# The router of a two-layer decoder step: order of the evictions, and nine constant matmuls a layer

## The chip, the cores and the metric

The kernel runs on one core of one Trainium2 chip. The metric is the device time of one execution in microseconds; lower is better. PE is the matmul engine (TensorE), DVE the vector engine, ACT the scalar engine, POOL GpSimd, SP the engine that issues most of the loads. TensorE's clock has two levels, 1.2 and 2.4 GHz; the profile gives the granted clock as a share of 2.4 GHz (1.00 or 0.50, a mean in between for a stretch that holds both).

## The reference

A decoder trunk of two layers works on 288 tokens (256 of a prompt, 32 of eight sample streams), 1024 channels wide, all in float32. Each layer has a recurrent mixer, a cross-attention into 256 memory tokens, and a mixture of experts; each is followed by a residual and a LayerNorm. The part around the change is the end of the attention and the router of the experts:

```python
x = layer_norm(DN_ALPHA * x + memory_attention(x, mem_k[l], mem_v[l], w_mq[l], w_mo[l]), ln_g[l, 1], ln_b[l, 1])
...
grp_logits = xt @ w_grp + b_grp                 # 4 groups, the best one is taken
e_logits = einsum('nd,gde->nge', xt, w_er) + b_er   # 8 experts of that group, the best two are taken
...
hid = silu(xt @ w_gate) * (xt @ w_up)           # for each expert, 1024 to 512
out = out + (hid * combine) @ w_down            # 512 to 1024
```

There are 32 experts in a layer, with 6 MB of weights each.

## The kernel before

One program holds a block for each engine; they meet by semaphores that count up. Tokens lie in three tiles: tiles 0 and 1 are the prompt (128 rows each), tile 2 the 32 sample rows. The router takes them in the order 2, 0, 1 (`ORDER`).

*From the projection to the logits.* PE's `project_out` multiplies the attention's output by its weights into PSUM banks 0 to 4. DVE's `norm` then takes each tile in order: residual, mean and variance (L1427, L1429), a first step (L1430), and, once ACT has given the reciprocal root of the variance (ACT's `norm`, L1163 and L1164), the second step (L1432), which raises `ln_done`. PE's `logits(l, t)` turns tile t with transposes into PSUM banks 6 and 7 (`run_jobs`, L641, two jobs for each tile, half the channels each), ACT copies each half to `XT` (`empty_jobs`, L1056), and PE multiplies `XT` by the router's weights (L908). A job may begin when the copy of the job two before it is done, and ahead of the last tile's logits PE waits for all the copies of the stage.

ACT works its instructions in the order in which they are written. Before, it does the roots of all three tiles (`norm(2 + 3 * l)`), and then all six copies.

*From the logits to the experts.* In `moe`, DVE picks group and experts from the logits in some 25 small steps (L1504 to L1516, `assigned`), PE sums up each token's rank in its expert (L917, `ranks`) and each expert's count (L920, `counts`), DVE builds a selection matrix from the ranks (L1533), and PE's `gather(0)` picks the tokens of the first four experts with 48 matmul instructions (L946) into PSUM banks 0 and 1.

*The experts.* Four experts make a gang, and eight gangs follow each other. The weights of a gang come in 12 units of 2 MB (four of w_gate, four of w_up, four of w_down). A ring of eight slots holds them. SP loads units 0 to 7 ahead of time, each as soon as its slot is free; unit n + 8 is loaded when PE has finished unit n (`unit_done`). On PE a unit of the first two kinds is 16 instructions (L966). Between units PE gathers the next gang's tokens (L946) and adds the last gang's output to the tokens (L929).

A float32 matmul is two instructions of PE; counts of instructions in the rows are therefore twice the counts of matmuls.

Of the kernel before, what the change touches and what calls it, by code (L numbers as in the profile page):

```python
# [54 lines left out]
def build(nc, I, O):  # L55

    _, SEQ, D = I["x_prompt"].shape
    DB, DS, _ = I["x_sample"].shape
    NA, _, HEADS, DK, HDV = I["state_hgrn"].shape
    NC_, GDV = I["state_gla"].shape[0], I["state_gla"].shape[4]  # L60
    DEPTH, _, MEM, MH, MHD = I["cache_mem_k"].shape
    GROUPS, EPG, _, DE = I["w_gate"].shape[1:]
    CW = I["conv_w"].shape[1]
# [4 lines left out]
    PT_ = SEQ // P  # L68
# [3 lines left out]
    HALF = 512  # L72
# [19 lines left out]
    def cols(t):  # L92
        return slice(t * P, t * P + ROWS[t])

    ctx = ExitStack()
    with ctx:
        sems = {}

        def S(name):
            if name not in sems:  # L100
                sems[name] = ctx.enter_context(nc.semaphore(name))
            return sems[name]

        def sb(name, shape, dt=F32):
            return ctx.enter_context(nc.sbuf_tensor(name, shape, dt))


        ones = sb("ones", [P, P])
# [12 lines left out]
        X = sb("X", [P, TT, D])  # L121
# [18 lines left out]
        ps = ctx.enter_context(nc.psum_tensor("ps", [P, 8, HALF], F32))  # L140
# [138 lines left out]
        jobs = {}  # L279
# [52 lines left out]
        def between(l, h, place):  # L332

            lo = sum(n for at, n in BETWEEN[l].items() if at < (h, place))
            return jobs["fill", l][lo:lo + BETWEEN[l].get((h, place), 0)]
# [25 lines left out]
        def count_at(name, l, n):  # L361

            return l * per_layer[name] + n
# [259 lines left out]
        def _(pe):  # L623
            mm, tr = pe.matmul, pe.transpose
# [182 lines left out]
            def attention(l):  # L807
# [88 lines left out]
                last.then_inc(S("os_ps"), 1)  # L896
                pe.wait_ge(S("oa_ready"), count_at("oa_ready", l, 3))

            def logits(l, t):
                stage = ("xt", 2 + 3 * l)  # L900
                xt = [j for j in jobs[stage] if j[1][1] == t]
                run_jobs(stage, xt)
                if t == PT_:
                    pe.wait_ge(S("router_in"), 16 * (GROUPS + 3) * (l + 1))
                for k in range(KC):
                    if k % 4 == 0:
                        pe.wait_ge(S("pipe_free"), xt[k // 4][0] + 1)
                    last = mm(ps[0:ROWS[t], 5, t * 64:t * 64 + GROUPS + NE], XT[:, k, cols(t)], router_w[:, k, :],  # L908
                              start=(k == 0), stop=(k == KC - 1))
                last.then_inc(S("logits"), 1)  # L910

            def moe(l):
                for t in ORDER:
                    logits(l, t)
                pe.wait_ge(S("assigned"), count_at("assigned", l, 1))
                for n, (by, at, upto) in enumerate(((upper, 0, TT), (ones, 1, TT - 1), (ones, 2, TT - 2))):
                    last = mm(ps[:, 4, at * NE:TT * NE], by[:], ASG[:, 0:upto, :].rearrange("p t e -> p (t e)"), start=(n == 0), stop=(n == TT - 1))  # L917
                last.then_inc(S("ranks"), 1)
                for u in range(TT):
                    last = mm(ps[:, 5, TT * NE:(TT + 1) * NE], ones[:], ASG[:, u, :], start=(u == 0), stop=(u == TT - 1))  # L920
                last.then_inc(S("counts"), 1)
                def scatter(it, part):

                    for n in part:
                        t, j = n // 2, n % 2
                        if n >= 2:
                            pe.wait_ge(S(f"acc{l}"), it * SCATTERS + (n - 1))
                        if t < PT_:
                            last = mm(ps[:, 7 - n % 2, :], PWT[:, cols(t)], Y[:, j * HALF:(j + 1) * HALF], start=True, stop=True)  # L929
                        else:  # L930

                            for q in range(4):
                                last = mm(ps[q * NS:(q + 1) * NS, 7 - n % 2, 0:D // 4], PWT[:, cols(t)],
                                          Y[:, q * (D // 4):(q + 1) * (D // 4)], start=True, stop=True)
                        last.then_inc(S(f"scat{l}"), 1)
# [99 lines left out]
        def _(act):  # L1035
# [11 lines left out]
            def empty_jobs(stage, some=None):  # L1047
                for n, (kind, name, c) in jobs[stage] if some is None else some:
                    act.wait_ge(S("pipe_full"), n + 1)
                    bank = ps[:, 6 + n % 2, :]  # L1050
                    l = stage[1]
                    m = MIX[l] if l < 2 else None
                    full = bank[:, 0:NT]
                    if kind == "xt":
                        src = bank.rearrange("p (k t) -> p k t", k=4)[:, :, 0:ROWS[name]]
                        ins = fn(XT[:, 4 * c:4 * c + 4, cols(name)], src, ACT.Copy)  # L1056
                    elif kind == "feat" and name[:2] == "mq":
                        ins = fn(QT[:, 4 * int(name[2]) + c, :], full, ACT.Copy, scale=float(MHD) ** -0.5)
                    elif kind == "feat" and name in ("bg", "cg", "h"):
                        ins = fn(m["conv"][("bg", "cg", "h").index(name)][:, c, :], full, ACT.Copy)  # L1060
                    elif kind == "feat" and name == "f":
                        ins = fn(m["b"][:, c, :], full, ACT.Copy)
                    elif kind == "feat" and name == "q" and l == 0:
                        ins = fn(m["q"][:, c, :], full, ACT.Silu)
                    elif kind == "feat" and name == "q":
                        ins = fn(m["q"][:, c, :], full, ACT.Copy, scale=float(DK) ** -0.5)
                    elif kind == "feat" and name == "k":
                        ins = fn(m["k"][:, c, :], full, ACT.Copy)
                    elif kind == "feat":
                        ins = fn(m["g"][:, 4 * (name == "g1") + c, :], full, ACT.Silu)  # L1070
                    elif kind == "gz":
                        ins = fn(gz[:], bank[0:RANK, 0:NT], ACT.Copy)
                    elif kind == "gk":
                        ins = fn(m["b"][:, c, :], full, ACT.Identity, bias=bgk2[:, c:c + 1])
                    elif kind == "tok":
                        at = HALF * (name == "v1")
                        if c < PT_:
                            ins = fn(m["v"][:, c, at:at + HALF], bank, ACT.Copy)
                        else:
                            for q in range(4):  # L1080
                                ins = fn(m["v"][0:NS, c, at + q * P:at + (q + 1) * P], bank[q * NS:(q + 1) * NS, 0:P], ACT.Copy)  # L1081
                    elif kind == "mt":
                        ins = fn(memT[:, 4 * c:4 * c + 4, name * P:(name + 1) * P], bank.rearrange("p (k t) -> p k t", k=4), ACT.Copy)  # L1083
                    elif kind == "memtok":
                        at = HALF * int(name[2])
                        dst = MK if name[:2] == "mk" else VP
                        ins = fn(dst[:, c, at:at + HALF], bank, ACT.Copy)
                    elif kind == "ct":
                        ins = fn(conv_tok, bank[0:2 + 2 * DB, :], ACT.Copy)
                    elif kind == "kt":  # L1090
                        ins = fn(KTP[:, 2 * c:2 * c + 2, :].rearrange("p c m -> p (c m)"), bank, ACT.Copy)
                    ins.then_inc(S("pipe_free"), 1)
# [64 lines left out]
            def norm(inst, tiles=range(TT)):  # L1157
                if inst % 3 == 0:
                    act.preload_act_table_set(EXP_AND_LN)
                for n in tiles:  # L1160
                    R = ROWS[ORDER[n]]
                    act.wait_ge(S("var_ready"), 3 * (inst - 1) + n + 1)
                    st.step(fn(mv[0:R, 2:3], mv[0:R, 1:2], ACT.Ln, bias=eps[0:R, 1:2]))  # L1163
                    st.tell(fn(mv[0:R, 3:4], mv[0:R, 2:3], ACT.Exp, scale=-0.5), S("std_ready"))  # L1164
# [84 lines left out]
            for l in range(DEPTH):  # L1249
                mixer(l)  # L1250
                norm(1 + 3 * l)
                empty_jobs(("fill", l), between(l, HEADS, 0))
                attention(l)
                norm(2 + 3 * l)
                empty_jobs(("xt", 2 + 3 * l))
                load_gb(3 + 3 * l)
                moe(l)
                norm(3 + 3 * l)
                if l + 1 < DEPTH:
                    empty_jobs(("xt", 3 + 3 * l))  # L1260
# [379 lines left out]
```

## Time and profile before

| | us |
|---|---|
| median of 3 runs | 1849.94 |
| lowest and highest run | 1848.97, 1851.25 |
| the profiled execution | 1850.28 |
| its span, first to last instruction | 1848.6 |
| mean granted TensorE clock over the span | 0.875 |
| PE busy | 1511.0 (82%) |
| DVE busy, ACT busy | 414.7 (22%), 259.7 (14%) |
| bytes read from memory over the span | 521.75 MB, mean 289 GB/s with the written ones |

A busy PE is not a PE at its peak: matmuls overlap and their ends are modelled. Shares over the whole span mix stages with different limits; layer 0's experts run from about 401 to 884 us, layer 1's from about 1340 to the end.

### The profile page before, as it was taken

How to read it: one execution, taken by the hardware profiler on the slowest of the kernel's cores; microseconds unless marked ns; L12 is line 12 of the kernel's file. 1: busy time of each engine (PE TensorE's matmuls, PEld its weight loads, DVE VectorE, ACT ScalarE, POOL GpSimd, SP SyncE). 2: the span in 40 equal slices, each digit the busy share in tenths (PEclk: the TensorE clock that was granted, in tenths of full speed). 3: DMA queues.
4: the chain of work that ended last, by engine and by line, in shares of the span. 5: the costliest groups of instructions: out<-in, count | busy, mean ns of one | idle time of the engine just before them, and what ended most of it. 6: DMA issues, size and time to landing. Idle time of an engine off the chain costs nothing.

```text
span 1848.6 us, 21660 instructions
## 1 busy us (share of the span) xinstructions
PE 1511.0 (82%) x9042; PEld 782.2 (42%) x9042; DVE 414.7 (22%) x954; ACT 259.7 (14%) x502; POOL 116.0 (6%) x266
## 2 busy tenths in 40 slices
PE   8999999879777777777699998998898667766773
PEld 6675457453322132213475554575553212221221
DVE  1135333241100110011411432323411011001104
ACT  2222113110000000000122211122100000000000
POOL 5212200000000000000030111000000000000000
PEclk9999999978877787778799888999778889888986
DMA  8334644948999999999532435358659999999992
GB/s 290 137 116 155 208 174 166 365 160 347 409 410 410 410 410 409 410 410 407 192 125 104 140 106 190 121 211 316 253 221 409 410 409 410 409 410 410 410 409 115
DMA packets 167249, 535.17 MB, mean 290 GB/s; under 512 B 5582, under 2 KB 23054, under 8 KB 167184
## 3 DMA queue, kind: packets, MB, share of 16 engines
q1 hardware_dynamic: 163296, 522.08, 73.2%
q0 software_dynamic: 2160, 5.89, 1.1%
q10 hardware_dynamic: 1728, 6.29, 0.9%
q8 instruction: 47, 0.77, 0.2%
q14 instruction: 18, 0.15, 0.0%
HBM read 521.75 MB, written 12.49 MB: 289 GB/s over the span
## 4 chain that ended last, share of the span: by engine, by line
PE 52%; DMA 30%; SPq 11%; DVE 3%; ACT 2%; issue 1%; ACTq 0%; DVEq 0%; POOL 0%
PE ps L648 12%; SPq L444 11%; DMA scr<-in_w_gate 8%; DMA W<-in_w_gate 7%; PE ps L703 6%; PE ps L682 6%; PE ps L966 6%; PE ps L946 5%; DMA scr<-in_w_up 4%; DMA MEMB<-in_w_gate 4%; DMA W<-in_w_down 3%; DMA W<-in_w_up 3%; PE ps L663 2%; PE ps L796 2%; PE ps L815 1%
## 5 line engine op out<-in xcount | busy, mean ns | idle before, releaser
L966 PE MATMUL ps<-W,scr 128*32 128x512 f32 x1536 | 234.4, 749 | 102.4 <-DMA W<-in_w_gate 57.4
L648 PE MATMUL ps<-XT,W 128*128 128x288 f32 x896 | 228.9, 419 | 3.5 <-ACT XT L1056 2.2
L648 PEld LDWEIGHTS ps<-XT,W 128*128 128x128 f32 x896 | 174.9, 196 | 54.2 <-ACT XT L1056 3.0
L1581 DVE TENSOR_TENSOR scr<-scr,ps 128x512 f32<-128x512 f32 x16 | 11.0, 687 | 746.7 <-PE ps L966 746.7
L946 PE MATMUL ps<-scr,X 128*128 128x128 f32 (+1 forms) x864 | 175.7, 338 | 0.0
L966 PE MATMUL ps<-scr 128*32 128x512 f32 x768 | 110.9, 706 | 73.0 <-DMA scr<-in_w_gate 29.3
L966 PEld LDWEIGHTS ps<-W,scr 128*32 128x32 f32 x1536 | 50.2, 125 | 258.9 <-issue 101.6
L946 PEld LDWEIGHTS ps<-scr,X 128*128 128x128 f32 (+1 forms) x864 | 135.7, 213 | 56.4 <-issue 28.7
L966 PE MATMUL ps<-MEMB,scr 128*32 128x512 f32 x768 | 116.3, 753 | 23.9 <-DMA MEMB<-in_w_gate 23.9
L682 PE MATMUL ps<-W,MEMB 128*128 128x512 f32 x256 | 116.5, 609 | 0.8 <-ACT MEMB L1083 0.8
L929 PE MATMUL ps<-scr 128*128 128x512 f32 x144 | 86.7, 723 | 2.4 <-ACT scr L1246 2.2
L966 PEld LDWEIGHTS ps<-scr 128*32 128x32 f32 x768 | 23.1, 116 | 146.8 <-DMA scr<-in_w_gate 43.9
L682 PEld LDWEIGHTS ps<-W,MEMB 128*128 128x128 f32 x256 | 49.5, 197 | 60.0 <-issue 57.8
L966 PEld LDWEIGHTS ps<-MEMB,scr 128*32 128x32 f32 x768 | 26.9, 130 | 102.1 <-issue 82.1
L703 PE MATMUL ps<-W,scr 128*128 128x512 f32 x128 | 59.9, 629 | 5.4 <-DVE scr L1395 5.4
L1561 DVE TENSOR_TENSOR scr<-scr,ps 128x512 f32<-128x512 f32 x72 | 49.5, 688 | 60.7 <-PE ps L929 60.7
L703 PE MATMUL ps<-W,XT 128*128 128x512 f32 x128 | 59.2, 623 | 1.5 <-ACT XT L1217 1.5
L1238 ACT ACT_TABLE_LOAD x16 | 20.5, 1283 | 283.4 <-PE ps L966 283.4
L929 PEld LDWEIGHTS ps<-scr 128*128 128x128 f32 x144 | 29.4, 237 | 61.4 <-issue 40.7
L1230 ACT ACTIVATE scr<-ps 128x512 f32<-128x512 f32 x18 | 10.7, 597 | 311.8 <-PE ps L966 292.7
L663 PE MATMUL ps<-W,XT 128*128 128x512 f32 x96 | 42.0, 594 | 1.2 <-ACT scr L1081 1.2
L1246 ACT ACTIVATE scr<-ps 128x1024 f32<-128x1024 f32 x16 | 16.4, 1023 | 185.3 <-PE ps L966 185.3
(286 smaller groups left out, 1335.3 us busy)
## 6 DMA issues: line engine op xcount, KB each, us to landing
W<-in_w_gate SPq DMA_DIRECT2D x32, 2048.0 KB, 23.7
W<-in_w_up SPq DMA_DIRECT2D x32, 2048.0 KB, 23.7
W<-in_w_down SPq DMA_DIRECT2D x32, 2048.0 KB, 23.8
scr<-in_w_gate SPq DMA_DIRECT2D x16, 2048.0 KB, 23.8
MEMB<-in_w_up SPq DMA_DIRECT2D x16, 2048.0 KB, 23.6
scr<-in_w_down SPq DMA_DIRECT2D x16, 2048.0 KB, 23.8
MEMB<-in_w_gate SPq DMA_DIRECT2D x16, 2048.0 KB, 23.5
scr<-in_w_up SPq DMA_DIRECT2D x16, 2048.0 KB, 24.0
```

Source lines behind the costliest of these rows:

```text
L444: sp.dma_start(ring_slot(l, n % RING).rearrange("p (j n) -> p j n", j=GANG), rows[:, e, :]).then_inc(S(f"ring{n % RING}_in{l}"), 16)
L648: last = mm(bank[:, 0:NT], w[:, k, c * P:(c + 1) * P], XT[:, k, :], start=(k == 0), stop=(k == KC - 1))
L663: last = mm(bank[:, :], XT[:, k, cols(c)], w[:, k, :], start=(k == 0), stop=(k == KC - 1))
L682: last = mm(bank, memT[:, k, c * P:(c + 1) * P], w[:, k, :], start=(k == 0), stop=(k == KC - 1))
L703: last = mm(ps[:, 2 * t + j, :], src[:, k, cols(t)], w[j][:, k, :], start=(k == 0), stop=(k == KC - 1))
L796: last = mm(ps[:, b // per % 2, (b % per) * nv:(b % per + 1) * nv], m["kexp"][:, b, :], m["v"][0:NS, 2, h * nv:(h + 1) * nv], start=True, ...
L815: last = tr(ps[:, j, (2 * c + i) * P:(2 * c + i + 1) * P], src[:, i, (2 * j + c) * P:(2 * j + c + 1) * P], ident)
L929: last = mm(ps[:, 7 - n % 2, :], PWT[:, cols(t)], Y[:, j * HALF:(j + 1) * HALF], start=True, stop=True)
L946: last = mm(ps[:, k // 4, (k % 4) * P:(k % 4 + 1) * P], pairs_of_x(t)[:, k // 2, :, k % 2], PG[0:ROWS[t], t, :, :].rearrange("p j c -> p ( ...
L966: last = mm(ps[j * CAP:(j + 1) * CAP, bank, :], x[:, k, j * CAP:(j + 1) * CAP], w[:, j, i, c * HALF:(c + 1) * HALF], start=(part % 4 == 0 ...
L1238: fn(SG, ps[:, 2, :], ACT.Silu).then_inc(S(f"sg{l}"), 1)
L1561: ins = tt(a, a, ps[:, bank, :], ALU.add)
```

## The change

ACT's order in each layer is altered: the roots of the first two tiles of the order (2 and 0), the four copies of these tiles, then the root of tile 1 and its two copies. On PE, a new helper `keep_warm(n)` issues n matmuls of the constant matrix `ones` by the first 512 columns of the normed tile 0, into PSUM bank 0; nothing reads what they write there, and `gather(0)` overwrites it. Nine of them are issued in each layer: one between the transposes and the logits of tile 0, one behind these logits, one between the (copied) transposes and the logits of tile 1, five behind these logits, and one behind the counts.

```diff
+            def keep_warm(n):
+
+                for _ in range(n):
+                    mm(ps[:, 0, :], ones[:], X[:, 0, 0:HALF], start=True, stop=True)
+
             def logits(l, t):
                 stage = ("xt", 2 + 3 * l)
                 xt = [j for j in jobs[stage] if j[1][1] == t]
                 run_jobs(stage, xt)
+                if t != PT_:
+                    keep_warm(1)
                 if t == PT_:
                     pe.wait_ge(S("router_in"), 16 * (GROUPS + 3) * (l + 1))
...
             def moe(l):
                 for t in ORDER:
                     logits(l, t)
+                    if t != PT_:
+                        keep_warm((1, 5)[t])
                 pe.wait_ge(S("assigned"), count_at("assigned", l, 1))
...
                 last.then_inc(S("counts"), 1)
+                keep_warm(1)
...
                 attention(l)
-                norm(2 + 3 * l)
-                empty_jobs(("xt", 2 + 3 * l))
+                by_tile = jobs["xt", 2 + 3 * l]
+                norm(2 + 3 * l, (0, 1))
+                empty_jobs(("xt", 2 + 3 * l), by_tile[:4])
+                norm(2 + 3 * l, (2,))
+                empty_jobs(("xt", 2 + 3 * l), by_tile[4:])
                 load_gb(3 + 3 * l)
                 moe(l)
```

`by_tile` lists the jobs in the order of the tiles (2, 0, 1), so its first four are those of tiles 2 and 0. `norm(..., (0, 1))` names places in the order, not tiles.

## Rows read from the trace of the kernel before

**Rows 1.** Chain that ended last, layer 0: start us, us, what
```profile
366.97 13.95 PE ps L703 x32
...
417.39 9.65 PE ps L966 x64
...
435.79 7.05 PE ps L966 x64
442.99 23.22 DMA W<-in_w_gate
```

**Rows 2.** Windows: length, PE busy (instructions), granted clock, DMA share, GB/s
```profile
380.83:385.08 4.25, 0.88 (x16) 1.00 0.76 240
385.08:388.49 3.41, 3.41 (x28) 0.50 0.79 326
388.49:395.32 6.83, 4.37 (x37) 1.00 0.47 149
395.32:421.32 26.00, 21.55 (x80) 0.50 0.01 2
426.97:435.72 8.75, 8.75 (x53) 1.00 1.02 410
424.00:875.88 451.88, 345.64 (x2057) 0.83 1.03 409
1320.33:1359.91 39.58, 32.70 (x137) 0.50 0.14 53
```

**Rows 3.** Timeline of PE, router of layer 0: start, us, what [idle before]
```profile
380.83 0.68 PE L641 MATMUL ps<-eye,X 32*128 32x32 f32 x8
384.88 0.97 PE L908 MATMUL ps<-router_w,XT 128*32 128x36 f32 x16 [3.37 <-ACT XT L1056]
385.78 1.97 PE L641 MATMUL ps<-eye,X 128*128 128x128 f32 x8
...
389.81 1.07 PE L641 MATMUL ps<-eye,X 128*128 128x128 f32 x8
391.62 1.98 PE L908 MATMUL ps<-router_w,XT 128*128 128x36 f32 x16 [0.74 <-ACT XT L1056]
398.79 0.74 PE L917 MATMUL ps<-scr,upper 128*128 128x96 f32 x2 [5.19 <-DVE scr L1516]
...
400.09 1.47 PE L920 MATMUL ps<-scr,ones 128*128 128x32 f32 x6
401.37 15.04 PE L946 MATMUL ps<-scr,X 128*128 128x128 f32 x48
```

**Rows 4.** Timeline of PE's weight loads: two of the projection, one of unit 1
```profile
349.73 0.34 PEld L703 LDWEIGHTS ps<-W,XT 128*128 128x128 f32 x1 [0.52 <-issue]
350.58 0.34 PEld L703 LDWEIGHTS ps<-W,XT 128*128 128x128 f32 x1 [0.52 <-issue]
...
420.80 0.20 PEld L966 LDWEIGHTS ps<-W,scr 128*32 128x32 f32 x4 [0.65 <-issue]
```

**Rows 5.** Timeline of ACT and DVE, router of layer 0
```profile
383.89 0.29 ACT L1163 ACTIVATE mv<-mv,eps 128x1 f32<-128x1 f32 x1 [6.34 <-DVE mv L1429]
...
384.45 0.45 ACT L1056 ACTIVATE XT<-ps 128x128 f32<-128x128 f32 x2
...
385.15 1.28 DVE L1432 SCALAR_TENSOR_TENSOR X<-X,mv,GB 128x1024 f32<-128x1024 f32 x1
...
387.79 0.60 ACT L1056 ACTIVATE XT<-ps 128x512 f32<-128x512 f32 x1 [0.26 <-PE ps L641]
```

**Rows 6.** Timeline of SP's loads: the first issue of each MoE stage's stream
```profile
421.32 2.91 SPq L444 DMA_DIRECT2D W<-in_w_down  x2
...
1359.91 2.91 SPq L444 DMA_DIRECT2D W<-in_w_down  x2
```

**Rows 7.** Timeline of PE, router of layer 1
```profile
1315.88 0.68 PE L641 MATMUL ps<-eye,X 32*128 32x32 f32 x8
...
1328.54 3.63 PE L908 MATMUL ps<-router_w,XT 128*128 128x36 f32 x16 [0.69 <-ACT XT L1056]
```

## The prediction

> **What bounds the kernel now.** I read the page first. Its slices show the DMA engines full at about 410 GB/s in two long stretches, and its chain shares put 30% of the span on weight transfers. So the chain of waits comes next: behind the first two batches of expert matmuls the chain leaves TensorE for the transfer of a weight unit [rows 1]. From there to the end of the layer the experts run as fast as weights arrive. The windows view says the same: from 424.00 to 875.88 us the DMA share is 1.03 at 409 GB/s [rows 2]. A MoE stage therefore ends a fixed time after its stream of weights starts, and nothing made faster inside the stream is worth anything.
>
> What starts the stream? Eight weight units are loaded ahead; the ninth load waits until PE has finished unit 0 and freed its slot. Between 395.32 and 421.32 us the DMA share is 0.01 [rows 2]: the memory system is idle while router and first gather run. SP issues the ninth unit at 421.32 us in layer 0 and at 1359.91 us in layer 1 [rows 6]. Counted from the start of the transposes of tile 2, right behind the output projection (380.83 and 1315.88 us, [rows 3, 7]), that is 40.49 and 44.03 us. Every microsecond taken out of these two stretches should come off the span.
>
> Third, the windows with the granted clock. TensorE is at 2.4 GHz when the projection ends, falls to 1.2 GHz at 385.08 us after a stretch with little but waiting, comes back at 388.49, falls again at 395.32 while DVE picks experts, and is at 1.2 GHz all through the first gather and unit 0 [rows 2]. In layer 1 it never comes back: 0.50 from 1320.33 to 1359.91 us [rows 2]. The same gather code at 2.4 GHz takes 8.75 us [rows 2]; here it takes 15.04 [rows 3]. Notice that the gather at 1.2 GHz keeps PE busy for 15 us and the clock doesn't rise, while the gather at 2.4 GHz is granted 2.4 GHz to its end. The level at which the gather begins decides its price.
>
> **The change part by part.** *Eviction order.* ACT now copies out the turned tiles 2 and 0 before the reciprocal root of tile 1. Before, tile 2's copy began only at 384.45 us, behind the root of 383.89, and the logits of tile 2 followed at 384.88 [rows 5, 3], though the transposes were done at 381.51. Now the copy follows the transposes, 0.45 us long: logits at +1.15 us instead of +4.05. What is put behind it: tile 1's root (0.56 us from 383.89 to the copy) waits for tile 0's second copy, and DVE's last step of tile 1 waits for the root. Tile 0's second copy ends at about +3.85 (below), so the root is there at +4.4; DVE could begin that step at +4.32 before (385.15) [rows 5]. At most 0.1 us late, and tile 1 is then ready at about +5.7, before PE wants it. ACT's two gain and bias loads stay behind the last copy, as before. No queue of SP or POOL is passed.
>
> *Nine constant matmuls.* Each is two PE instructions of 512 columns: 32 such instructions take 13.95 us at 2.4 GHz, so 0.87 us a matmul [rows 1]; at 1.2 GHz instructions of this kind start 0.85 us apart, so 1.70 us [rows 4]. No row shows what they do to the clock. The nearest are the projection, gated at 2.4 GHz throughout, and the thin logits, behind which it fell. Bounds: below, all hidden and the clock held; above, all at 1.70 us and no effect. I take 0.87, nearest to the projection, since their instructions are the same form.
>
> *The sum*, as time after the first transpose of tile 2, with 2.4 GHz prices: transposes 0.68, copy 0.47 with its start: +1.15. Logits of tile 2, 0.97: +2.1. Transposes of tile 0, 1.07 as tile 1's were at that clock: +3.2. One constant matmul: +4.05; it covers the second copy (0.60 us, which began 0.04 us behind the transposes, [rows 5, 3]), done at +3.85, so most of it is free. Logits of tile 0, 1.98: +6.05. A matmul, uncovered: +6.9. Transposes of tile 1, 1.07, then the wait for the copy, 0.64: +8.6. A matmul, uncovered, because PE waits for all copies of the stage before it: +9.5. Logits of tile 1, 1.98: +11.45. DVE's expert choice, 5.19 (393.60 to 398.79): +16.65; five matmuls, 4.35, fit inside and leave 0.85 idle. Ranks and counts took 2.58 at 1.2 GHz up to the gather (398.79 to 401.37); scaled as the transposes, 1.07 to 1.97, that is 1.4, plus one matmul 0.87: +18.9. Gather 8.75: +27.65. The pause before unit 0, 0.98: +28.65. Unit 0 at 7.05 for four units, 1.76: +30.4. SP issues 0.52 us later (from 417.39, four rounds of instructions 0.85 us apart end unit 0 at 420.8, where a weight load of unit 1 stands; the issue comes at 421.32): +30.9. [rows 1 to 6]
>
> So 9.6 us come off in layer 0 (40.5 to 30.9) and 13.1 in layer 1 (44.0 to 30.9), 22.7 together. The profiled execution took 1850.28 us (span 1848.6), 0.34 above the median of 1849.94, which is inside the spread of the runs. 1850.28 less 22.7 is 1827.6; I say 1827.5. Of the 22.7, some 12.4 is the two gathers, 3.3 unit 0 in both layers, and the rest the router.
>
> Where the sum could be off in this case: three single matmuls a layer lie on the path (behind tile 0's logits, ahead of tile 1's, ahead of the gather). Wholly hidden, six times 0.87 less: 1822.4. At 1.70 each, six times 0.83 more: 1832.5.
>
> *A rule that speaks against it.* Layer 0 ran tile 0's transposes in the stretch from 385.08 to 388.49 us, granted 1.2 GHz; they are most of PE's time there, and right behind it 2.4 GHz was granted. Tile 1's then took 1.07 us at that clock [rows 2, 3]. The Trainium skill, TensorE: Matmul & The Clock Gate, Part 4 (PE-mode transpose), says that transposes don't count as activity to the clock gate in the way matmuls do. By that rule the clock would drop among the transposes in spite of the single matmuls, and the time would be that of the second rival; by the rows it is my sum. The trace agrees with it in neither of the two places of layer 0. Layer 1, with the same transposes, stayed at 1.2 GHz [rows 2, 7], which is why that rival is kept.
>
> **The rivals.**
>
> *The clock drops once more just ahead of the gather.* Between the five matmuls and the gather PE has an idle 0.85 us and thin ranks and counts, the like of which let the clock fall at 395.32 [rows 2]. Then the gather costs 15.04 instead of 8.75, unit 0 3.4 instead of 1.76 and the steps before it up to 1 more: 9 us for a layer. Against it: the five are right ahead and one more behind. In one layer: 1836.5, chance 0.15. In both: 1845.5, chance 0.04.
>
> *Transposes and logits don't hold the clock, the five bring it back.* Then logits cost 3.63 each instead of 1.98 [rows 7], transposes 1.97 instead of 1.07, three singles 1.70, and the five end 1 to 2 us behind DVE: 8.5 us a layer against my sum, 1844.5. Speaking for it: layer 1 before. Chance 0.05.
>
> *Slower: constant matmuls don't act on the clock.* All nine then cost 1.70 us. In layer 1, relative to before: three singles on the path 5.1; the five 8.5 against DVE's 5.19, so 3.3; the one behind the counts 1.7; less 2.9 for the earlier copy: 7.2 later. Layer 0 also loses the 2.4 GHz that it had at tile 1 (0.9 for transposes, 1.65 for logits): 9.8. Together 17, so 1867. It decides when the five end with the clock still at 1.2 GHz. Against it: the projection's matmuls, of the same form, are granted 2.4 GHz. Chance 0.05.
>
> *No change*: the stream of weights is not moved by what precedes it, because some other wait (the loop count, the slots) starts it. The issue 0.52 us behind unit 0 in layer 0 speaks against it. 1850, chance 0.03.
>
> **How the numbers follow.** My case has 0.68: 1827.5, its own range 1822 to 1833. With the drop in one layer, to 1838, 0.83 is held, so the range is 1822 to 1838. A measurement of this kernel can tell about 0.2%, 3.7 us, from no change. Faster: 0.68, 0.15, 0.04 and 0.05, 0.92. Same 0.03, slower 0.05.
>
> **What would show it.** The granted clock reads 1.00 from the end of the projection to unit 0 in both layers; the first gathers take 8.8 us; tile 2's copy starts within 0.1 us of its transposes; SP issues the ninth unit 31 us behind them, and the stream then lasts as long as before. A first gather of 15 us would make the size wrong; ranks that start behind the last of the five would make the fit of the five wrong; a stream start moved without the span would make the whole chain of argument wrong.

## The result, and the profile after

| | us |
|---|---|
| before, median of 4 runs | 1850.6 |
| changed, median of 4 runs (lowest, highest) | 1824.72 (1821.36, 1827.08) |
| ratio, 95% interval | 0.9862 [0.9846, 0.9879] |
| profiled execution, before and changed | 1850.28, 1827.08 |
| its span, before and changed | 1848.6, 1825.4 |
| mean granted clock over the span | 0.875, 0.926 |

The changed kernel is 1.4% faster. One execution of the kernel with the new order alone, below, took 2392.61 us at a mean granted clock of 0.547; the ratio given there is formed without it. The windows of the changed kernel come first (length, PE busy with instructions, granted clock, DMA share, GB/s):

```profile
381.51:385.00 3.49, 3.22 (x38) 1.00 0.70 194
385.00:392.00 7.00, 6.20 (x45) 1.00 0.87 321
392.00:399.81 7.81, 6.99 (x27) 1.00 0.10 34
399.81:408.63 8.82, 8.81 (x49) 1.00 0.01 2
...
1308.82:1339.13 30.31, 27.43 (x175) 1.00 0.29 105
...
409.79:413.20 3.41, 3.41 (x20) 0.50 0.00 0
416.00:868.20 452.20, 319.55 (x2052) 0.90 1.03 409
```

Where [rows 2] fell to 1.2 GHz twice in layer 0 and for good in layer 1, the clock is now granted 2.4 GHz from the projection to the end of the first gather in both layers. One fall is left: at 409.79 us, in layer 0, just as unit 0 begins. Layer 1 holds to the start of the stream. The stream itself is as long as it was: 452.20 us at 409 GB/s against 451.88.

The timeline of PE in the router of layer 0, changed kernel, answers to [rows 3]:

```profile
381.51 0.68 PE L641 MATMUL ps<-eye,X 32*128 32x32 f32 x8
382.46 0.68 PE L915 MATMUL ps<-router_w,XT 128*32 128x36 f32 x16 [0.27 <-ACT XT L1066]
383.07 1.09 PE L641 MATMUL ps<-eye,X 128*128 128x128 f32 x8
384.00 1.02 PE L902 MATMUL ps<-X,ones 128*128 128x512 f32 x2
384.86 1.87 PE L915 MATMUL ps<-router_w,XT 128*128 128x36 f32 x16
...
387.50 1.04 PE L641 MATMUL ps<-eye,X 128*128 128x128 f32 x8
389.34 1.13 PE L902 MATMUL ps<-X,ones 128*128 128x512 f32 x2 [0.80 <-ACT XT L1066]
...
392.00 4.54 PE L902 MATMUL ps<-X,ones 128*128 128x512 f32 x10
397.37 0.46 PE L926 MATMUL ps<-scr,upper 128*128 128x96 f32 x2 [0.82 <-DVE scr L1529]
...
399.81 8.82 PE L956 MATMUL ps<-scr,X 128*128 128x128 f32 x48
409.61 5.34 PE L976 MATMUL ps<-W,scr 128*32 128x512 f32 x32 [0.99 <-issue]
```

L902 is the constant matmul. PE's wait ahead of tile 2's logits has shrunk from 3.37 to 0.27 us, the five matmuls leave 0.82 us idle before the ranks, and the first gather takes 8.82 us instead of 15.04. In layer 1 the gather and unit 0 stand at:

```profile
1327.12 8.82 PE L956 MATMUL ps<-scr,X 128*128 128x128 f32 x48
1336.92 3.64 PE L976 MATMUL ps<-W,scr 128*32 128x512 f32 x32 [0.99 <-issue]
```

The issues of SP that start the streams, from its timeline, answer to [rows 6]:

```profile
413.41 2.16 SPq L444 DMA_DIRECT2D W<-in_w_down  x2
...
1339.13 2.01 SPq L444 DMA_DIRECT2D W<-in_w_down  x2
```

Counted from tile 2's transposes (381.51 and 1308.82 us) that is 31.90 and 30.31 us, where it was 40.49 and 44.03. Below, "stream" with a plus sign is this distance, from the same two rows of each kernel. The two distances are 8.59 and 13.72 us shorter, 22.31 together, and the span 23.2. By the starts of PE's instructions, 12.5 of the 22.31 us are the two gathers with the pause behind them (from 16.02 and 16.05 to 9.80 each), 1.9 are unit 0 up to SP's issue (from 3.93 in both layers to 3.80 and 2.21), and 8.0 are the stretch ahead of the gather (from 20.54 and 24.05 to 18.30 each). The rest is outside the change: the chain's last pieces of each kernel hold most of it. Before:

```profile
1814.20 2.67 PE ps L966 x16
...
1817.98 5.73 PE ps L929 x8
```

and after:

```profile
1793.55 1.97 PE ps L976 x16
...
1796.62 3.89 PE ps L939 x8
```

The last unit and the last scatter, which nobody changed, ran 2.5 us faster, with the clock up in this execution (granted 1.00 in the scatter, 0.64 before); 1.5 us went the other way ahead of the two routers.

### The profile page after: what moved, and what is told of

It reads as the page before. It is cut to its first block, busy times and chain, and to the rows that moved or that the text cites. A ratio compares the mean times of both kernels' runs of the same rounds, so it can differ in the third digit from the quotient of the medians.

```text
span 1825.4 us, 21730 instructions
## 1 busy us (share of the span) xinstructions
PE 1458.4 (80%) x9078; PEld 755.6 (41%) x9078; DVE 413.3 (23%) x954; ACT 259.1 (14%) x502; POOL 116.0 (6%) x266
## 4 chain that ended last, share of the span: by engine, by line
PE 52%; DMA 32%; SPq 9%; DVE 3%; ACT 2%; issue 1%; ACTq 0%; DVEq 0%; POOL 0%
PE ps L648 12%; SPq L444 9%; DMA scr<-in_w_gate 8%; PE ps L703 7%; PE ps L682 6%; DMA W<-in_w_gate 6%; PE ps L976 6%; DMA scr<-in_w_up 5%; PE ps L956 4%; DMA W<-in_w_up 4%; DMA MEMB<-in_w_gate 4%; DMA W<-in_w_down 3%; PE ps L663 2%; PE ps L796 2%; PE ps L815 1%
## 5 line engine op out<-in xcount | busy, mean ns | idle before, releaser
L976 PE MATMUL ps<-W,scr 128*32 128x512 f32 x1536 | 213.7, 692 | 126.0 <-DMA W<-in_w_gate 68.3
L956 PE MATMUL ps<-scr,X 128*128 128x128 f32 (+1 forms) x864 | 158.7, 314 | 0.0
L956 PEld LDWEIGHTS ps<-scr,X 128*128 128x128 f32 (+1 forms) x864 | 122.7, 194 | 50.7 <-issue 16.5
L976 PE MATMUL ps<-MEMB,scr 128*32 128x512 f32 x768 | 102.5, 675 | 29.6 <-DMA MEMB<-in_w_gate 29.6
L976 PEld LDWEIGHTS ps<-scr 128*32 128x32 f32 x768 | 23.2, 121 | 166.4 <-DMA scr<-in_w_gate 44.6
L939 PE MATMUL ps<-scr 128*128 128x512 f32 x144 | 73.9, 619 | 3.8 <-ACT scr L1256 2.3
L939 PEld LDWEIGHTS ps<-scr 128*128 128x128 f32 x144 | 23.0, 189 | 47.1 <-issue 25.1
## 6 DMA issues: line engine op xcount, KB each, us to landing
W<-in_w_down SPq DMA_DIRECT2D x32, 2048.0 KB, 23.9
```

The lines of the kernel that those rows point to most:

```text
L956: last = mm(ps[:, k // 4, (k % 4) * P:(k % 4 + 1) * P], pairs_of_x(t)[:, k // 2, :, k % 2], PG[0:ROWS[t], t, :, :].rearrange("p j c -> p ( ...
L976: last = mm(ps[j * CAP:(j + 1) * CAP, bank, :], x[:, k, j * CAP:(j + 1) * CAP], w[:, j, i, c * HALF:(c + 1) * HALF], start=(part % 4 == 0 ...
```

## The experiments

The level of the clock in them is read from windows as above; "falls at" and "rises at" are the borders at which the granted clock changes between 1.00 and 0.50. Ratios are to runs of the kernel before on the same chip.

**The new order alone.** No constant matmul:

```diff
-                if t != PT_:
-                    keep_warm(1)
...
-                    if t != PT_:
-                        keep_warm((1, 5)[t])
...
-                keep_warm(1)
```

> Only ACT's order is changed, no constant matmul. Theory A (the gain is the clock level at which gather and unit 0 begin, and the constant matmuls hold it): the router ends some 3 us earlier in each layer, but the clock falls while DVE chooses experts, the first gathers take 15.0 us, SP issues the ninth unit at +37 to +41 us behind tile 2's transposes; time 1841 to 1846. Rival B (the earlier copies alone close the idle gap and keep the clock up): gathers 8.8 us, stream at +28 to +31, time 1820 to 1826.

Measured: 1842.0 us, ratio 0.9966 [0.9952, 0.9979]; streams at +38.65 and +39.71. PE's timeline of layer 1:

```profile
1318.70 1.94 PE L641 MATMUL ps<-eye,X 128*128 128x128 f32 x8 [0.88 <-DVE X L1440]
1321.33 3.63 PE L913 MATMUL ps<-router_w,XT 128*128 128x36 f32 x16 [0.69 <-ACT XT L1061]
...
1332.71 15.04 PE L951 MATMUL ps<-scr,X 128*128 128x128 f32 x48
```

and its window from the fall to the next rise, 0.24 us ahead of the stream:

```profile
1318.29:1352.42 34.13, 26.87 (x104) 0.50 0.14 51
```

The idle gap of 3.37 us is closed (0.27 is left) and the clock falls all the same, before DVE even starts to choose: in layer 1 behind tile 0's logits, in layer 0 during tile 1's (at 386.45). That is earlier than theory A had put it, but the gathers and the size are A's. Rival B, that the order alone keeps the clock, is out. The order is worth 6.4 us by itself. The row of 1318.70 shows something else: without the single matmul, PE waits 0.88 us for DVE at tile 1.

**The matmuls alone.**

```diff
-                norm(2 + 3 * l, (0, 1))
-                empty_jobs(("xt", 2 + 3 * l), by_tile[:4])
-                norm(2 + 3 * l, (2,))
-                empty_jobs(("xt", 2 + 3 * l), by_tile[4:])
+                norm(2 + 3 * l)
+                empty_jobs(("xt", 2 + 3 * l))
```

> The nine constant matmuls, ACT's old order. Theory A: PE idles 3.4 us ahead of tile 2's logits and the clock falls there as before; the single matmuls cost 1.70 us until it rises, at the latest within the five; the gathers take 8.8 us. Stream at +34 to +42 us, time 1830 to 1847 by how soon it rises. Rival B: without the new order nothing is won, 1850, with the matmuls' own time on top 1850 to 1867.

Measured: 1834.88 us, ratio 0.9934 [0.9914, 0.9954]; streams at +34.94 and +36.60. PE in layer 0:

```profile
384.99 0.96 PE L915 MATMUL ps<-router_w,XT 128*32 128x36 f32 x16 [3.37 <-ACT XT L1066]
...
387.65 1.51 PE L902 MATMUL ps<-X,ones 128*128 128x512 f32 x2
...
403.87 8.82 PE L956 MATMUL ps<-scr,X 128*128 128x128 f32 x48
```

The old 3.37 us wait is back and the clock falls at 385.20, nearly where it fell before; it is up again at 388.62 and then stays up to the stream, where [rows 2] show it falling again at 395.32. The rise itself is no effect of the matmuls in layer 0, for [rows 2] have one at 388.49. In layer 1 the clock used to stay down; here it is up at 1320.45 and stays up through the gather, and falls once more at 1344.3, as unit 0 begins (unit 0's first 32 instructions then take 5.20 us instead of 3.64). So the constant matmuls do act on the clock, which the slower rival denied: they hold it in both layers, and in layer 1 they bring it back. Two of the seven executions took 1842.84 and 1843.36, 8 us more than the others; the traced one isn't among them, so what they lost isn't shown.

Order and matmuls alone give 6.4 and 13.5 us, 20 together, where the whole change gives about 25. Each alone leaves a stretch at 1.2 GHz that the other closes. The gathers need the matmuls and not the order: they ran at 2.4 GHz with the old order too.

**Without the five.**

```diff
-                        keep_warm((1, 5)[t])
+                        keep_warm((1, 0)[t])
```

> The change without the five matmuls behind tile 1's logits (the four single ones stay). Theory A: the clock falls in the five microseconds in which DVE chooses experts; ranks, the single matmul behind the counts, the gather (15.0 us) and unit 0 run at 1.2 GHz; stream at +40 us, time 1842 to 1846. Rival B: the clock holds from the router on, gathers 8.8 us, time as with the whole change, 1821 to 1827.

Measured: 1837.4 us, ratio 0.9938 [0.9922, 0.9955]; streams at +32.73 and +40.09. PE in both layers, and the windows of layer 0:

```profile
399.47 2.05 PE L902 MATMUL ps<-X,ones 128*128 128x512 f32 x2
401.31 9.26 PE L956 MATMUL ps<-scr,X 128*128 128x128 f32 x48
...
1328.43 14.90 PE L956 MATMUL ps<-scr,X 128*128 128x128 f32 x48
```

```profile
381.04:395.77 14.73, 9.59 (x79) 1.00 0.64 216
395.77:402.60 6.83, 5.71 (x19) 0.50 0.01 4
402.60:410.57 7.97, 7.97 (x44) 1.00 0.00 0
```

With only the single matmuls the router holds 2.4 GHz, and the clock falls while DVE chooses, in both layers, as theory A says. What A had not foreseen is layer 0: the one matmul behind the counts, run at 1.2 GHz, was followed by a rise at 402.60, 1.3 us into the gather. In layer 1 the same instructions were not. Layer 0's stream starts 7.4 us ahead of layer 1's, which fits a time 4.6 us below A's lower end.

**Without the four singles.**

```diff
-                if t != PT_:
-                    keep_warm(1)
...
-                        keep_warm((1, 5)[t])
+                        keep_warm((0, 5)[t])
...
-                keep_warm(1)
```

> The new order and the five matmuls; the four single ones left out. Theory A in its simple form (transposes and logits hold the level once the idle gap is gone, the five carry it over the expert choice): three uncovered matmuls of 0.87 us a layer are saved, stream at +28 us, time 1818 to 1823. Rival C (transposes and logits don't hold it, as the page's rule on transposes says; the single matmuls are needed): 1.2 GHz in the router, the five bring it back, stream at +34 to +38 us, time 1832 to 1841. Rival D (the single matmul behind the counts is needed): the router at 2.4 GHz, but the clock falls ahead of the gather, 15.0 us, time 1835 to 1842.

Measured: 1828.38 us, ratio 0.9909 [0.9881, 0.9937], single executions from 1826.65 to 1843.13; streams at +33.36 and +33.41. PE in layer 0, and its windows:

```profile
386.82 1.94 PE L641 MATMUL ps<-eye,X 128*128 128x128 f32 x8 [0.88 <-DVE X L1442]
389.45 3.63 PE L913 MATMUL ps<-router_w,XT 128*128 128x36 f32 x16 [0.69 <-ACT XT L1063]
392.88 6.43 PE L902 MATMUL ps<-X,ones 128*128 128x512 f32 x10
...
400.91 8.82 PE L953 MATMUL ps<-scr,X 128*128 128x128 f32 x48 [0.35 <-DVE scr L1543]
```

```profile
386.46:396.70 10.24, 9.19 (x29) 0.50 0.47 165
396.70:410.35 13.65, 12.69 (x66) 1.00 0.01 2
410.35:413.76 3.41, 3.04 (x16) 0.50 0.00 0
```

Rival C by mechanism: without the singles the clock falls behind tile 0 in both layers, and the five bring it back, at 396.70, before they end. A's simple form is out. So is rival D: the matmul behind the counts is missing here as well, and the gather ran at 2.4 GHz in both layers. C's price was too high: I had 34 to 38 us for the streams, and they stand at 33.4. The five run over DVE's choice by only 0.9 us (its last step ends at 398.21, the ranks begin at 399.15) and lead straight into the ranks, so the gather begins at +19.8 instead of +18.3. The other 1.5 us is not the router's: in both layers the clock falls once more as unit 0 begins (at 410.35 and 1335.4). The Trainium skill, TensorE: Matmul & The Clock Gate, Part 4 (PE-mode transpose), holds that transposes don't count to the clock gate as matmuls do. This run agrees as far as it goes, since it can't tell the transposes from the thin logits beside them. The rise at 388.49 in [rows 2] speaks against the Trainium skill without settling it: in the stretch from 385.08 us up to it, transposes take 1.8 us and logits the rest.

**Without the last single.**

```diff
                 last.then_inc(S("counts"), 1)
-                keep_warm(1)
```

> The change without the single matmul behind the counts. If that matmul carries the clock into the gather, the clock falls at or soon behind the ranks: a gather of up to 15.0 us or at least unit 0 at 1.2 GHz in some layers and executions, median 1827 to 1838. If the five alone suffice, the gather begins 0.7 us earlier in each layer and the median is 1.0 to 1.5 below the whole change's.

Measured: 1836.58 us, ratio 0.9934 [0.9915, 0.9953]; streams at +38.28 and +38.27. PE in layer 0, and the windows of both layers:

```profile
395.75 15.06 PE L955 MATMUL ps<-scr,X 128*128 128x128 f32 x48 [0.92 <-DVE scr L1545]
```

```profile
395.10:415.58 20.48, 18.84 (x68) 0.50 0.01 1
1326.94:1347.42 20.48, 19.05 (x68) 0.50 0.01 1
```

This is the prediction's first rival, called up by taking away one matmul: the clock falls 0.65 us before the gather in layer 0 and 0.44 us in layer 1, and both gathers run at 1.2 GHz throughout. They don't begin any earlier, as the other case had it: the gather waits 0.92 us for DVE and starts 18.30 us behind tile 2's transposes, with the matmul (399.81 less 381.51) and without it (395.75 less 377.45). So one hidden matmul in each layer is worth 12.6 us of the whole change's gain (medians of 1836.58 and, over twelve executions, 1824.0), as long as the other eight stand as they do. By itself it isn't needed: the run without all four singles lacks it too, and its gathers held 2.4 GHz. There PE idles 0.35 us between the five and the gather, here 0.82 and 0.92. Whether that idle time decides was not tested.

**Ten instead of five.**

```diff
-                        keep_warm((1, 5)[t])
+                        keep_warm((1, 10)[t])
```

> Ten matmuls instead of five behind tile 1's logits: 8.7 us against DVE's 5.2, so the ranks begin 3.5 us later in each layer with the clock held. If the start of the weight stream sets the end, both streams start 3.5 us later and the time is 7.0 us above the whole change's, 1830 to 1833. If the stream doesn't hang on the router (rival: something else starts it), the time doesn't move, 1823 to 1826.

Measured: 1828.48 us, ratio 0.9893 [0.9871, 0.9915]; streams at +33.27 in both layers. PE in layer 0, and the windows of layer 0 from the transposes to the stream and of the stream:

```profile
391.82 8.83 PE L902 MATMUL ps<-X,ones 128*128 128x512 f32 x20
400.48 0.36 PE L926 MATMUL ps<-scr,upper 128*128 128x96 f32 x2
...
402.68 8.71 PE L956 MATMUL ps<-scr,X 128*128 128x128 f32 x48
```

```profile
381.32:414.59 33.27, 31.21 (x185) 1.00 0.28 95
...
417.10:870.50 453.40, 313.74 (x2064) 0.93 1.03 409
```

The streams start 4.3 us later in sum than in the profiled execution of the whole change (66.54 against 62.21), and the median is 4.5 us above the 1824.0 that twelve executions of the whole change have. All four executions lie above all twelve of the whole change (1827.27 is the lowest here, 1827.08 the highest there). So the end follows the start of the streams, about one to one as far as the scatter lets it be told; the rival that they don't hang on the router is out. My 7.0 was too much: the streams come 3.0 us later where the clock holds (33.27 against 30.31), not 3.5, and 1.4 in layer 0, where the whole change's profiled execution lost time at unit 0 and this one doesn't.

**One matmul moved, one added.** The single of tile 1 goes ahead of PE's wait for the copies, and one more, into bank 3, fills the pause before unit 0:

```diff
-            def run_jobs(stage, some=None):
+            def run_jobs(stage, some=None, warm=0):
...
+                keep_warm(warm)
                 if stage[0] != "fill" and (some is None or some and some[-1][0] + 1 == number(stage)):
...
-                run_jobs(stage, xt)
-                if t != PT_:
-                    keep_warm(1)
+                run_jobs(stage, xt, int(t != PT_))
...
                 gather(0)
+                keep_warm(1, 3)
```

> The single matmul of tile 1 is issued before PE's wait for the copies instead of behind it (it fits into the 0.80 us of that wait), and one more fills the 0.99 us pause between the first gather and unit 0, into bank 3. The first saves 0.8 us a layer; the second keeps unit 0 at 2.4 GHz, where the clock fell at its start in layer 0 of the whole change (1.6 us). Together 1.6 to 4.8 us below the whole change: 1820 to 1823.

Measured: 1826.2 us, ratio 0.9877 [0.9856, 0.9898]; streams at +29.45 in both layers. PE in layer 0, and the windows of both layers:

```profile
385.55 1.02 PE L903 MATMUL ps<-X,ones 128*128 128x512 f32 x2
...
404.87 1.12 PE L903 MATMUL ps<-X,ones 128*128 128x512 f32 x2
405.93 3.64 PE L976 MATMUL ps<-W,scr 128*32 128x512 f32 x32
```

```profile
378.69:408.14 29.45, 28.36 (x177) 1.00 0.34 118
1302.22:1331.67 29.45, 28.36 (x177) 1.00 0.31 108
```

By the trace the moved matmul does what it was to do, 0.85 us less in each layer, and the clock doesn't fall at unit 0. That the added matmul keeps it up isn't shown, since layer 1 of the whole change holds it without one. The time did not show a gain. Beside it on the same chip stood the whole change:

> The whole change once more on the same chip as the three others, as their measure: 1821 to 1828, gathers 8.8 us, streams at +30 to +32 us.

It measured 1823.54 us, ratio 0.9866 [0.9844, 0.9889], streams at +31.78 and +30.31 (the clock fell at 404.88, again as unit 0 began). So both were taken once more:

> The version with the moved and the added matmul once more, since its streams start 3.2 us earlier in all (29.45 us in both layers against 31.78 and 30.31) but its median was not lower. If the rest of the program only scatters, its median over all executions comes out 2 to 4 us below the whole change's, near 1821; if the gain is given back somewhere, the medians stay equal within 1 us or it stays above.

Measured: 1825.25 us, ratio 0.9866 [0.9837, 0.9895], streams at +29.46 and +29.44.

> The whole change on the same chip, as the measure for the run beside it: 1819 to 1827, median near 1824.

Measured: 1823.45 us, ratio 0.9871 [0.9847, 0.9895], streams at +30.30 in both layers. Over all executions the median is 1825.8 us for the altered version (8) and 1824.0 for the whole change (12); single executions run from 1818.8 to 1827.4. What the streams gain, 1.7 to 3.3 us, is no larger than what the rest of the program scatters, and no gain can be told. It stays open whether some of it is given back elsewhere. The whole change remains the fastest that was measured.

## Why the prediction was right

Predicted were 1827.5 us (1822 to 1838), faster with 0.92; measured 1824.72.

- *What sets the end* was right: the start of the weight stream. It starts 22.31 us earlier in sum (22.7 predicted), the stream keeps its length, and delaying it by 4.3 us cost 4.5 (by the medians).
- *The eviction order*: tile 2's logits at +1.15 predicted, +0.95 measured. Tile 1 was not held up: with the order alone its transposes began at +5.76 behind DVE (5.7 predicted), and here PE comes to them at +5.99.
- *The router's steps* were 0.9 us too long up to tile 1's transposes (+5.99 instead of +6.9), mostly because I added up durations, and the instructions overlap at their ends in the trace: from start to start tile 2's logits take 0.61 us instead of 0.97, tile 0's 1.70 instead of 1.98.
- *The single matmuls* were priced right (0.86 to 0.96 us to the next start in the router, against 0.87), but not their cover. I had the one behind tile 0's logits uncovered; most of it fills a wait for DVE that would be there anyway (0.88 us in the run with the order alone). The one behind the counts is covered as well: the gather doesn't begin earlier without it. My sum left out that DVE must finish the selection matrix before the gather. That 2.25 us for ranks, counts and matmul came so near to the measured 2.44 was luck. The one ahead of tile 1's logits is uncovered as predicted: moving it saved 0.85 us a layer.
- *The five* took 4.54 us in DVE's time and left 0.82 us; predicted 4.35 and 0.85.
- *The gathers*: 8.82 us against 8.75, beginning at +18.3 against +18.9.
- *Unit 0* is the term that was mis-sized. I had it at 2.4 GHz in both layers, worth 3.3 us; it gave 1.9. In layer 0 the clock fell as it began in two of the three profiled executions of the whole change, at a cost of 1.5 to 1.6 us (streams at +31.9 and +31.8 instead of +30.3).
- *Layer by layer* 9.6 and 13.1 us were predicted, 8.6 and 13.7 measured. That the two sums agree to 0.4 us is partly luck: unit 0 in layer 0 cost 1.6 us more than I had, and the gathers began 0.6 us earlier in each layer.
- *The first rival*, a fall just ahead of the gather, did not come about in the change, but the run without the last single matmul has it in both layers. It cost 8.0 us of stream in layer 1 (38.27 against 30.31), where I had 9: the 6.2 of the gather and 1.7 of unit 0 are there, the steps ahead of the gather cost nothing. Of what I had put against it, the five ahead were not enough without the one behind the counts.
- *The second rival*, transposes and logits that don't hold the clock, has its mechanism right when the single matmuls are absent. Its price of 8.5 us a layer was not measured, for it counted three singles at 1.70 us that this run doesn't have; there the gather came 1.5 us later. With the single matmuls it does not occur.
- *The slower rival* falls: the clock rose behind a constant matmul in layer 1 of the run with the matmuls alone, and among the five in both layers of the run without the singles. The trace of the kernel before had a sign of it that I passed over: the projection that starts at 347.86 us begins at a granted 0.50 and has 1.00 from 351 us on.
- The 2.8 us between prediction and median are not in the two routers, where the trace is 0.4 us short of the sum; the profiled execution itself took 1827.08. They lie in the rest of the program, and what takes them isn't shown. It may be more than scatter: in all three comparisons the medians fall by 25 to 26 us, and the streams by 22.3 to 23.9.

Most of the gain therefore comes from the clock level at the first gather and unit 0 (14.3 of 22.3 us of stream), and the rest from the stretch ahead of them, which is shorter by the clock and by the new order (6.4 us alone). Only order, singles and five together gave all of it, but not every part is needed for the gather's level: it held without the new order, and without all four singles, and was lost without the last single alone. How 1.2 GHz is entered in detail is not settled, as the layers of one and the same execution differ.

## What to carry to other kernels

Where a transfer-bound stage is started by a short stretch of thin or waiting PE work, read the granted clock in that stretch: dense matmuls that nothing reads, put where PE waits anyway, can pay several times over. These were all of one form, 512 columns wide; no run tried another. Take them away one at a time, since one that looks spare may be what carries the level into the expensive step, and take them away in groups too, since what one is worth hangs on the others. Judge by the start of the stream in the trace, for the total's scatter hides effects of 2 or 3 us.

## What the runs showed of the hardware that was not expected

- The same gather code begun at 1.2 GHz took 14.90 us in layer 1 and 9.26 us in layer 0 of one execution (the run without the five): whether the clock rises early in such a gather differs from place to place.
- A fall of the clock can come at unit 0 although the gather before it ran at 2.4 GHz to its end (409.79 us in the changed kernel). Over all profiled executions, of thirteen first gathers that ended at 2.4 GHz with nothing in the pause behind them, five were followed by such a fall (layer 0 of the changed kernel twice, layer 1 with the matmuls alone, both layers without the singles). With a matmul in the pause none of four was, which is too few to call the matmul the cause.
- The span less the two stretches up to the streams, all of it code that no run altered, lies between 1755.0 us (1817.1 less 62.09, whole change, second time) and 1765.0 (1823.9 less 58.90, altered version, second time). The clock's level at the last scatter alone makes 1.8 us of such differences (3.89 and 5.73 us).
